# Where the moving operands of the matmuls begin in SBUF: a two-block transformer on one core

## The reference

```python
for i in range(2):
    m, mc = adaln(c, ada_w[i], ada_b[i]), adaln(c_ctx, ada_w[i], ada_b[i])
    h, hc = half_ffn(h, m, 0, ...), half_ffn(hc, mc, 0, ...)      # 1024 -> 2 x 2816 -> 1024
    u, uc = modulated_norm(h, g[2], m, 3), modulated_norm(hc, g[2], mc, 3)
    y, yc = diff_attention_mixer(...) if i == 0 else gqa_axial_mixer(...)
    h = gated_residual(h, y, g[3], m, 3, 1.0)
    h = half_ffn(h, m, 6, ...)
    if i == 0: hc = half_ffn(gated_residual(hc, yc, ...), mc, 6, ...)
```

## Time and profile before

| | |
|---|---|
| median of 3 runs | 2419.28 us (2418.53 to 2421.22) |
| span of the profiled execution | 2419.5 us |
| mean granted TensorE clock | 0.997 |
| TensorE busy | 2384.9 us, 99% |
| VectorE busy | 1600.1 us, 66% |
| ScalarE busy | 1063.2 us, 44% |
| DMA | 346.53 MB, mean 143 GB/s |

### The profile page before, as it was taken

The page is one execution under the profiler, slowest core; times in us unless marked ns, Lnnn a source line. Parts: engine busy times, 40 slices in busy tenths (PEclk is TensorE's granted clock), DMA queues, the critical chain, the costliest instruction groups (busy, mean ns, idle before and its releaser), DMA issues.

```text
span 2419.5 us, 36353 instructions
## 1 busy us (share of the span) xinstructions
PE 2384.9 (99%) x14712; PEld 2059.6 (85%) x14712; DVE 1600.1 (66%) x2899; ACT 1063.2 (44%) x1882; POOL 0.2 (0%) x4
## 2 busy tenths in 40 slices
PE   9999999999999999999999999999999999999998
PEld 5888888976788888888888888899998998999997
DVE  7776775477587677377623357655586776877767
ACT  4222324455552223252223245644556556555663
POOL 0000000000000000000000000000000000000000
PEclk9999999999999999999999999999999999999999
DMA  6554552211125455215522212245534443444432
GB/s 275 207 195 188 202 198 70 88 53 53 71 91 197 186 198 203 87 55 207 207 107 90 102 70 88 111 157 181 191 142 157 175 140 127 167 169 158 157 123 88
DMA packets 48408, 346.53 MB, mean 143 GB/s; under 512 B 5361, under 2 KB 5489, under 8 KB 6769
## 3 DMA queue, kind: packets, MB, share of 16 engines
q1 hardware_dynamic: 48242, 344.21, 38.3%
HBM read 343.14 MB, written 1.05 MB: 142 GB/s over the span
## 4 chain that ended last, share of the span: by engine, by line
PE 92%; DVE 5%; ACT 2%; issue 1%; DMA 0%; SPq 0%; DVEq 0%; ACTq 0%
PE ps L484 26%; PE ps L485 25%; PE ps L486 25%; PE ps L826 1%; PE ps L828 1%; PE ps L827 1%; DVE w_lo L2119 1%; PE ps L873 1%; PE ps L1030 1%; PE ps L654 1%; ACT w_hi L1430 1%; PE ps L679 1%; PE ps L1056 1%; PE ps L859 1%; PE ps L608 1%
## 5 line engine op out<-in xcount | busy, mean ns | idle before, releaser
L1430 ACT ACTIVATE w_hi<-ring 128x1024 fp32r<-128x1024 f32 x494 | 523.4, 1060 | 1052.5 <-PE ps L486 988.9
L2119 DVE TENSOR_TENSOR w_lo<-ring,w_hi 128x1024 fp32r<-128x1024 f32 x494 | 603.5, 1223 | 422.8 <-ACT w_hi L1430 419.5
L484 PE MATMUL ps<-u_hi,w_hi 128*128 128x512 f32 (+1 forms) x1856 | 656.8, 354 | 4.8 <-DVE u_lo L2192 2.3
L485 PE MATMUL ps<-u_lo,w_hi 128*128 128x512 f32 (+1 forms) x1856 | 648.6, 349 | 0.0
L486 PE MATMUL ps<-u_hi,w_lo 128*128 128x512 f32 (+1 forms) x1856 | 648.4, 349 | 0.0
L484 PEld LDWEIGHTS ps<-u_hi,w_hi 128*128 128x128 f32 x1856 | 348.4, 188 | 60.9 <-issue 7.7
L485 PEld LDWEIGHTS ps<-u_lo,w_hi 128*128 128x128 f32 x1856 | 348.5, 188 | 47.3 <-issue 0.5
L486 PEld LDWEIGHTS ps<-u_hi,w_lo 128*128 128x128 f32 x1856 | 348.6, 188 | 45.5
L484 PE MATMUL ps<-uh,w_hi 128*128 128x256 f32 x1136 | 321.9, 283 | 2.9 <-DVE w_lo L2119 1.7
L2107 DVE CUSTOM_DVE_ANT_0 waste<-ring,condb,cols 128x1024 f32<-128x1024 f32 x260 | 322.3, 1279 | 0.1
L486 PE MATMUL ps<-uh,w_lo 128*128 128x256 f32 x1136 | 315.4, 278 | 0.0
(11 more groups left out here) (364 smaller groups left out, 2686.6 us busy)
## 6 DMA issues: line engine op xcount, KB each, us to landing
ring<-in_wk SPq DMA_DIRECT2D x317, 1024.0 KB, 4.8
mix<-in_wk SPq DMA_DIRECT2D x3, 1024.0 KB, 16.2
yT<-in_wk SPq DMA_DIRECT2D x2, 1024.0 KB, 7.8
hT<-in_x SPq DMA_DIRECT2D x1, 2048.0 KB, 13.1
htabs<-in_htabs SPq DMA_DIRECT2D x1, 1088.0 KB, 7.3
out_t<-uT SPq DMA_DIRECT2D x2, 512.0 KB, 2.6
trig<-in_trig SPq DMA_DIRECT2D x3, 256.0 KB, 7.5
wuk<-in_uk SPq DMA_DIRECT2D x2, 256.0 KB, 5.1
```

Of the source, the lines that this page charges most:

```text
L484: mm(bank, hi, x_hi, start=first, stop=False, skip_group_check=skip)
L485: mm(bank, hi, x_lo, start=False, stop=False, skip_group_check=skip)
L1430: f(half_hi(K, 0, HALF), ringed(n, K % 2 * HALF, (K % 2 + 1) * HALF), ACT.Copy).then_inc(whi_ready, 1)
L2119: tt(half_lo(K, 0, HALF), ringed(HALF_SLOT[K], K % 2 * HALF, (K % 2 + 1) * HALF), half_hi(K, 0, HALF).bitcast(F32), ALU.subtract).then_inc ...
```

## The change

A tile's distance is the number of bytes from `w_hi` to it, modulo 256. The change places the split activations at chosen distances, each 8 bytes past a multiple of 64: `u_hi` and `u_lo` at 8, `h_hi`, `h_lo`, `uh2` and `ul2` at 72. It takes the next address at which the multiple of 32 below the wanted distance is met and leaves the first two columns of the tile unused. Tiles placed behind them move by up to some hundred bytes. Nothing else changes.

```diff
+LINE = 256
+U_APART = 8
+H_APART = 72
+SECOND_APART = 72
...
         ring = place("fixed", "ring", NRING * SLOT)
+        first_half = at["fixed"]
         w_hi = place("fixed", "w_hi", NW * HALF, F32R)
...
-        phases = at["fixed"]
+
+        def apart(place, distance):
+
+            return place + (distance - (place - first_half)) % LINE
+
+        def place_apart(region, name, cols, distance):
+
+            at[region] = apart(at[region], distance // 32 * 32)
+            n = distance % 32 // 4
+            return place(region, name, cols + n, F32R)[:, n:n + cols]
+
+        phases = apart(at["fixed"], U_APART // 32 * 32)
...
-        u_hi = place("first", "u_hi", KC * TT, F32R)
-        u_lo = place("first", "u_lo", KC * TT, F32R)
+        u_hi = place_apart("first", "u_hi", KC * TT, U_APART)
+        u_lo = place_apart("first", "u_lo", KC * TT, U_APART)
...
-        h_hi = place("ffn", "h_hi", NH * TT, F32R)
-        h_lo = place("ffn", "h_lo", NH * TT, F32R)
+        h_hi = place_apart("ffn", "h_hi", NH * TT, H_APART)
+        h_lo = place_apart("ffn", "h_lo", NH * TT, H_APART)
...
-        uh2 = place("second", "uh2", KC * S, F32R)
-        ul2 = place("second", "ul2", KC * S, F32R)
+        uh2 = place_apart("second", "uh2", KC * S, SECOND_APART)
+        ul2 = place_apart("second", "ul2", KC * S, SECOND_APART)
```

## The result

The changed kernel takes 2472.22 us (median of 4 runs, 2470.51 to 2472.74); the kernel before took 2418.95 (4 runs, 2418.53 to 2421.22). The ratio is 1.0219, with a 95% interval of 1.0205 to 1.0234: 53 us slower, where 59 us faster was predicted, and outside the range. The profiled execution has a span of 2468.7 us, so 49.2 us more than the one of before is what its trace can explain.

The account below looks back on a forecast made before the run. TensorE was taken to bound the kernel, by matmul count times distance between starts. -43.4 - 17.4 + 1.5 = -59.3 us gave 2360 us; likeliest case 2344 to 2382, the 8-in-10 range reaching to 2440.

Parts of the forecast that it names:

- The view of the bound: Whole kernel: TensorE, busy 2384.9 of 2419.5 us, sets the time as number of matmuls times distance between starts.
- Part 1: The 4824 matmuls with 512 columns: beat falls from 229.0 to 220.0 ns, 9.0 ns less each, -43.4 us.
- The lower bound of 213.3: Matmuls with 512 columns: fastest beat is the columns alone, 213.3 ns, a gain of 75.7 us.
- bound above of one step of 4.3 ns: Matmuls with 512 columns: at worst one more step between the two 256-column beats, a loss of 20.7 us.
- Part 2: Matmuls with 256 columns (u, uh, h): all go to the quick beat, -9.1, -7.3 and -1.0, together -17.4 us.
- the bound above of 10.4: Matmuls with 256 columns: at worst all go to the slow beat, 10.4 us more than now.
- Part 3: What moves unaimed: value projections, branches, ACT and DVE instructions put at 0, landings at +1.5 us.
- +3.7 as the bound: Value projections, 864 matmuls with exchanged roles: +3.7 us if they fell to the slow beat; taken as 0.
- +1.5 us for landings: First five slots and crow, landing by DMA in tiles moved from 64 to 32: slower landing, +1.5 us taken.
- (c): Rival, column matmuls and value projections: starts 8 bytes off the grid cost 4.3 ns each, 34.8 us, 2454 us; chance 0.20.
- the note on 16-byte cachelines: Column matmuls: a start 8 bytes past a line touches 129 lines instead of 128, 1.7 ns each, 21 us, 2440.
- The reading that the moving stream and the next load get in each other's way: TensorE matmuls: both read SBUF and addresses decide how much they hinder each other; extra of 15.7 ns at 512 columns.

Follow-up runs that it names:

- m3 trains: Bare matmul trains without the reference's computation, repeated twelve times behind differing float32 matmuls; 256 columns at distance 192 gave 113.3 ns in 8 of 12, 117.8 in 4.
- by_stage: Against the kernel before: split activations at distance 0 in the first five sub-layers, 64 in the last and in the second block; 2416.18 us, ratio 0.9982.
- all_eight: Against the kernel before: weights and split activations both begin 8 bytes off, so each distance stays 64; 2489.04 us, ratio 1.0296.

## Why the prediction was wrong

**The view of the bound held.** The time is the number of matmuls times the distance between starts, and placement does change that distance: counts times differences give 57.0 us, where the span's 49.2 us more and the 10.4 us less of work between make 59.6.

**Part 1 is the step that failed.** "I take the undisturbed beat as the columns plus the smallest extra seen, 6.7 ns: 220.0 ns". In its place stand 232.8 ns with u and 235.5 with h, so 3385 x 3.8 + 1368 x 6.65 = +22 us instead of -43.4. Two things were assumed there. The first, that the extra of a 256-column matmul is a floor that 512 columns can reach: of 256 places none is below 226.7, an extra of 13.3. The second, that leaving distance 64 leads towards the floor: only 2.2 ns were above the best, 4824 x 2.2 = 10.6 us in all, and most places are worse. No run supports 220; it was a number made by carrying one shape's extra over to another. The lower bound of 213.3 was wrong for these operands in the same way. A bound above of one step of 4.3 ns was passed by h's 6.65.

**Part 2 failed too.** All 256-column matmuls were to go to the quick beat of 113.4, -17.4 us; they went to 120 to 121, beyond the slow beat: +31.0 us, three times the bound above of 10.4. How many of them were slow before was read rightly from the mean durations: the starts give 117.7 ns for u, 115.5 for uh and ul, 114.5 for h. But the two beats of the earlier trace rows were taken as disturbed and undisturbed. They are two ways in which one placement can run: in the m3 trains what ran before chose between them, in by_stage h changed to the slow one at its old distance. Other placements have other beats.

**Part 3 was nearly right.** The value projections were put at 0 with +3.7 as the bound, and lost 2.7. The branches lost 1.4 where -2.5 to 0 was said. ScalarE, VectorE, the landings and the wait for weights: 0, as the run with moved neighbours shows for the whole (1.0004). The +1.5 us for landings wasn't needed. The taps of L2741 begin 8, 12 and 16 bytes into a row of `pad`, not 4, 8 and 12; two of three are off the grid of 16 all the same, and nothing hangs on the third.

**The rivals.** (c) had the sign, for a mechanism that doesn't hold. It asked for a cost per start off the grid of 16 bytes, one step of 4.3 ns: 34.8 us, against 53.3 measured. But 128 is on the grid and costs 21 to 24 us, and 8 bytes cost 5.8 ns at distance 8 against distance 0, 5.8 at 72 against 64, and 11.1 when the weights stand 8 off as well (240.0 against 228.9). By the note on 16-byte cachelines in the Trainium skill's "SBUF — State Buffer" the estimate was 1.7 ns; the runs show more off the grid, and as much again on it, so that rule doesn't account for the time.

The reading that the moving stream and the next load get in each other's way was said not to be shown. The runs bear out that the starts of both matter and that the load's length shifts the beat, but a load of 109 ns instead of 188 doesn't take the extra away, so what collides, if anything does, stays open. The Trainium skill, "TensorE: Matmul & The Clock Gate", Part 2, gives a back-to-back gap of 215.7 ns at 512 columns and two independent read ports. The bfloat16 trains agree (215.8 to 216.3, flat over the starts); the fp32r trains don't (226.7 to 240).

**What stays open.** Why a start of fp32r operands costs up to 13 ns above the best; what sets which of its beats a stretch runs at, with 256 columns and, in all_eight, with 512; and why two kernels (u alone at 8, all_eight) spread over 21 and 17 us. Executions that hold different beats for different shares of the time would do that, but one trace of each kernel can't show it. The bank and the identity of the tiles are excluded as causes; the length of the load and the number of columns shift the beat without explaining it.

## What to carry to other kernels

Before a placement is changed for speed, run bare trains of the kernel's own matmuls (its type, its widths, its order) at the candidate starts. Here 1.5 ms of such trains gave the 512-column beats of all kernels but one (all_eight) to within 1 ns. They did not give the 256-column beats. So counts times beats forecast losses of 17, 23, 36 and 79 us where about 24, 22, 27 and 68 came, and gains of 12, 8 and 5 us where 0, 0 and 4 came: good for telling bad places from good ones, hardly for choosing among the good. Trains that repeat with something else ahead of them show whether a place has one beat or two. Don't take a beat of one shape for the floor of another, nor two beats in a trace for "disturbed" and "free". And look for how good the present place is among all: here only 7 other places of 64 were as good or better, so that the blind move lost 53 us where the best one found won 4.

## What the runs showed that was not expected

With fp32r operands the beat of 512 columns depends on where both operands begin, down to steps of 4 bytes, and the six distances tried again 256 bytes further gave the same: 226.7 to 240.0 ns. By the moving operand's start modulo 16 (weights at 0, means over 16 places) it is 232.0 at 0, 237.8 at 4, 233.2 at 8 and 229.6 at 12, the same order with the weights at 4, 12 and 16; so a start 12 bytes off was on average better than an aligned one. bfloat16 showed none of it at six distances.

A train of 256 columns keeps either of two beats, 113.3 or 117.8 ns, to its end, at one and the same placement. A few matmuls ahead of it decide which. In the kernel all_eight the 512-column matmuls, too, ran at 230 to 231 ns in the first layer and at 240.0 in the second, at one placement.
